# The three passes of a split matrix product, taken with the low weights first

## The chip, the cores and the metric

The kernel runs on one core of one Trainium2 chip. Its time is that of one execution on the device in microseconds (us); lower is better. TensorE (PE) multiplies, VectorE (DVE) and ScalarE (ACT) work on elements, GpSimd (POOL) does very little here, and the DMA queues are fed by SyncE (SP) and in part by ScalarE.

## The reference, cut to what matters

Two transformer-like blocks work on 256 tokens of width 1024 in float32. The first has two layers, and each of them is

```
h = modulate(rms_norm(x, norm_mix), shift1, scale1)
q, k, v, hy, g = split(h @ w_in)
x_mix = (sig(g_a) * (attention(q, k, v) @ w_o_attn) + sig(g_h) * (hyena(hy) @ w_o_hyena)) @ w_out
x = x + gate1 * x_mix
g, u = split(modulate(rms_norm(x, norm_ffn), shift2, scale2) @ w_gate_up)
x = x + gate2 * ((silu(g) * u) @ w_down)
```

In the first layer 256 context tokens take the same way beside the 256 tokens, so that a product there has 512 columns; in the second layer it has 256. The second block has a mixer (`w_in_2`, `w_out_2`), a cross attention (`w_xq_2`, `w_xk_2`, `w_xv_2`, `w_xo_2`) and 32 experts, of which each token takes two.

## The kernel before, in words

Every weight of the dense products is read once, as 128x128 blocks, 8 blocks (a unit of 512 KB) per DMA, into a ring of six slots. A dense product is made of float32r matmuls, and each float32 operand is split into two float32r parts, a high one and a low one. For a unit of weights ScalarE copies the high part into `his` (line 431, three slots), and VectorE then subtracts it from the unit in place, which leaves the low part in `ring_r` (line 439). The activations have been split in the same way: `HH_r` and `H_r` are the high and low part of most inputs, `VT_r` and `YF_r` those of the input of `w_down`; other tiles, `area_r` and `KF_r` among them, serve for the remaining ones. In the names of the profile the first name behind the arrow is the moving tile (activations) and the second the stationary tile (weights): `bank<-HH_r,his_r` is high weights with high activations, `bank<-H_r,his_r` high weights with low activations, `bank<-HH_r,ring_r` low weights with high activations.

The product of one 128x128 block is then a **trio** of matmuls that add into the same PSUM bank; low with low is left out. Each matmul has a weight load (LDWEIGHTS, PEld) of its own. Three functions write such trios:

- `pe_block` (line 460): one output bank, 4 or 8 blocks one after the other, the activations changing with each block. It makes the products of `w_in`, `w_o_attn`, `w_o_hyena`, `w_out`, `w_gate_up`, and most of the second block's.
- `pe_pair` (line 475): two output banks side by side, so that two trios in turn use the same activations. It makes the first two heads and the first pair of gate and up of each layer.
- `three` in `pe_down` (line 1608): four output banks, so that four trios in turn use the same activations (the blocks n = 0 to 3 of one k).

Four other places write their trios by themselves (lines 927, 1833, 1974, 2104).

Before a trio TensorE waits until the activations are there and until the low part of the unit is there (`ve_lo`, which VectorE counts up at line 439, after the high part). Nothing is waited for inside a trio. When the last matmul of a block product has ended, `pe_products` goes up; that lets ScalarE and VectorE take the bank, lets ScalarE overwrite the slot of `his` (line 431), and lets SyncE load the next unit into the slot of the ring. The order of the instructions on each engine is written out by hand in the program. Column sums by ones (lines 499 and 909) and small products stand between some blocks.

The experts at the end are plain float32 products from other slots. A branch behind them (`overflowing`) is taken only when an expert has more than 32 tokens: it then loads all experts a second time, 32 x 12 loads of 512 KB through a single slot (lines 2690 and following).

Of the kernel before, what the change touches and what calls it, by code (L numbers as in the profile page):

```python
# [267 lines left out]
def two_blocks_kernel(nc, T):  # L268
    ctx = ExitStack()
    with ctx:  # L270
# [145 lines left out]
        def hi_slot(n):  # L416
            return his[:, (n % NHI) * UF:(n % NHI + 1) * UF]

        def lo_slot(i):
            r = i % NS  # L420
            return ringr[:, r * UF:(r + 1) * UF]
# [21 lines left out]
        def pe_block(pe, key, out, name, l, b0, nk, moving, ready, step=1, n=1, turned=False, signals_end=True):  # L443
            for k in range(nk):
                w, i = stream.block(name, l, b0 + step * k, n)
                ready(k)
                if name in SPLIT:
                    pe.wait_ge(*ve_lo.at(nth[i]))
                    c = ((b0 + step * k) % UB) * P
                    whi, wlo = hi_slot(nth[i])[:, c:c + n * P], lo_slot(i)[:, c:c + n * P]  # L450
                    xhi, xlo = moving(k)
                    three = ((whi, xhi), (whi, xlo), (wlo, xhi))
                else:
                    pe.wait_ge(*stream.arrived(i))
                    three = ((w, moving(k)),)
                for m, (a, b) in enumerate(three):
                    end = k == nk - 1 and m == len(three) - 1
                    if turned:
                        a, b = b, a
                    ins = pe.eng.matmul(out, a, b, start=k == 0 and m == 0, stop=end)  # L460
                stream.spent[i] = (pe_products, key)
            if signals_end:
                ins.then_inc(*pe_products.up(*key))


        def pe_pair(pe, blocks, name, l, moving, ready):
            for k in range(8):
                ready(k)
                xhi, xlo = moving(k)
                for key, out, b0 in blocks:  # L470
                    w, i = stream.block(name, l, b0 + k)
                    pe.wait_ge(*ve_lo.at(nth[i]))
                    whi, wlo = hi_slot(nth[i])[:, k * P:k * P + P], lo_slot(i)[:, k * P:k * P + P]
                    for m, (a, b) in enumerate(((whi, xhi), (whi, xlo), (wlo, xhi))):
                        ins = pe.eng.matmul(out, a, b, start=k + m == 0, stop=k == 7 and m == 2)  # L475
                    stream.spent[i] = (pe_products, key)
                    if k == 7:
                        ins.then_inc(*pe_products.up(*key))

        def unit(name, l, b):  # L480
            return where[name, l, b // UB]
# [6 lines left out]
        def pe_open(pe, site, read_by=None, root_read_by=None):  # L488
            banks.hold(read_by or (ve_norm, ("used", site)), "sum", site)
            rsts.take(root_read_by or (pe_sums, ("spread", site)), site)  # L490
# [13 lines left out]
        def pe_added(site):  # L504
            for n in range(7):
                squares.take((ve_squares, ("added", site, max(n, 1))), site, n)
            squares.take((pe_sums, (site, 7)), site, 7)

        def pe_sum_seven(pe, site, cols):
            pe.wait_ge(*ve_squares.at("added", site, 6))  # L510
            pe.wait_ge(*banks.emptied("sum", site))
            for tb in range(cols // P):
                ins = pe.eng.matmul(banks.ap("sum", site)[:, tb:tb + 1], seven[:, tb * P:(tb + 1) * P], ones[:, 0:1], start=tb == 0,
                                    stop=False)
            ins.then_inc(*pe_sums.up(site, "seven"))

        def pe_sum_last(pe, site, cols):
            pe.wait_ge(*ac_squares.at(site, 7))
            for tb in range(cols // P):
                ins = pe.eng.matmul(banks.ap("sum", site)[:, tb:tb + 1], squares.ap(site, 7)[:, tb * P:(tb + 1) * P], ones[:, 0:1],  # L520
                                    start=False, stop=tb == cols // P - 1)
            ins.then_inc(*pe_sums.up(site, 7))
# [9 lines left out]
        def pe_spread(pe, site, cols, give=True):  # L532
            pe.wait_ge(*landed["con"])
            pe.wait_ge(*ve_norm.at("rstd", site))
            for tb in range(cols // P):
                ins = pe.eng.matmul(banks.ap("sum", site)[:, tb * P:(tb + 1) * P],
                                    rsts.ap(site)[:, tb:tb + 1].to_broadcast([P, P]), ident, start=True, stop=True)
            ins.then_inc(*pe_sums.up("spread", site))
            if give:
                banks.give("sum", site)  # L540


        def pe_idle(pe, site, n):
            out = banks.take((pe_sums, ("idle", site)), "idle", site)
            pe.wait_ge(*banks.emptied("idle", site))
            pe.wait_ge(*gp_start.at("ones"))
            for i in range(n):
                ins = pe.eng.matmul(out[:, 0:P], ones[:, :], ones[:, :], start=True, stop=True)
            ins.then_inc(*pe_sums.up("idle", site))
# [325 lines left out]
        def tokens(l):  # L875
            return 256 if l else 512
# [13 lines left out]
        def pe_head(pe, l, i):  # L890
            b, cols, _, _ = heads(l)[i]
            out = head_bank(pe, l, i)
            pe_block(pe, ("head", l, i), out[:, 0:cols], "w_in", l, 8 * pos[b], 8, lambda k: (HH[:, k, 0:cols], HL[:, k, 0:cols]),
                     lambda k: pe.wait_ge(*ve_norm.at("low", f"mix{l}", k)))
# [684 lines left out]
        def down_site(l):  # L1579
            return "final" if l else "mix1"  # L1580
# [12 lines left out]
        def cut_place(tile, m, t):  # L1593
            return tile[:, m % 4, 0:t]

        def pe_down(pe, l):
            t, site = tokens(l), down_site(l)
            pe_added(site)

            def three(half, k, n):  # L1600
                m, b = 22 * half + k, 88 * half + 4 * k + n
                u, c = unit("w_down", l, b), (b % UB) * P
                hi, lo = cut_place(VTR, m, t), cut_place(YFR, m, t)
                pe.wait_ge(*ve_cut.at("ff", l, m))
                pe.wait_ge(*ve_lo.at(nth[u]))
                whi, wlo = hi_slot(nth[u])[:, c:c + P], lo_slot(u)[:, c:c + P]
                for i, (w, x) in enumerate(((whi, hi), (whi, lo), (wlo, hi))):
                    ins = pe.eng.matmul(banks.ap("ff", l, 4 * half + n)[:, 0:t], w, x, start=k == 0 and i == 0, stop=k == 21 and i == 2)  # L1608
                return ins, u

            for half in range(2):
                for n in range(4):
                    banks.hold((ve_out, ("ff", l, 4 * half + n, t // 256 - 1)), "ff", l, 4 * half + n)
                for n in range(4):
                    pe.wait_ge(*banks.emptied("ff", l, 4 * half + n))
                for k in range(19 if half else 22):
                    for n in range(4):
                        ins, u = three(half, k, n)
                        if k == 21 and n < 3:
                            ins.then_inc(*pe_products.up("ff", l, half, n))  # L1620
                    ins.then_inc(*pe_products.up("down", l, half, k))
                    stream.spent[u] = (pe_products, ("down", l, half, k))
                if half:
                    for n in range(4):
                        for k in range(19, 22):
                            ins, u = three(half, k, n)
                            stream.spent[u] = (pe_products, ("down", l, 1, 21))
                        ins.then_inc(*pe_products.up("ff", l, half, n) if n < 3 else pe_products.up("down", l, 1, 21))
                for n in range(4):
                    banks.give("ff", l, 4 * half + n)  # L1630
            if l == 0:
                pe_open(pe, site)
                pe_sum_seven(pe, site, t)
                pe_sum_last(pe, site, t)
                pe_spread(pe, site, t)
                pe_idle(pe, site, 14)
# [1400 lines left out]
```

## Time and profile before

| | |
|---|---|
| Median of 3 executions | 2082.93 us (2081.61 to 2088.01) |
| Profiled execution, first to last instruction | 2084.6 us |
| TensorE busy | 1889.2 us, 91%, 14150 matmuls |
| VectorE busy | 1156.6 us, 55% |
| ScalarE busy | 903.5 us, 43% |
| DMA | 428.01 MB |

The busy time of TensorE counts from the first start to the last end of matmuls that overlap each other, so the time from one start to the next is shorter than the "mean ns" of one. No figure stands beside the span for what lies around it. Of the three executions without the profiler one is above the span and two are below it.

### The profile page before, as it was taken

How to read it: one execution, taken by the hardware profiler on the slowest of the kernel's cores; microseconds unless marked ns; L12 is line 12 of the kernel's file. 1: busy time of each engine (PE TensorE's matmuls, PEld its weight loads, DVE VectorE, ACT ScalarE, POOL GpSimd, SP SyncE). 2: the span in 40 equal slices, each digit the busy share in tenths (PEclk: the TensorE clock that was granted, in tenths of full speed). 3: DMA queues.
4: the chain of work that ended last, by engine and by line, in shares of the span. 5: the costliest groups of instructions: out<-in, count | busy, mean ns of one | idle time of the engine just before them, and what ended most of it. 6: DMA issues, size and time to landing. Idle time of an engine off the chain costs nothing.

```text
span 2084.6 us, 33760 instructions
## 1 busy us (share of the span) xinstructions
PE 1889.2 (91%) x14150; PEld 1554.0 (75%) x14150; DVE 1156.6 (55%) x1898; ACT 903.5 (43%) x1532; POOL 16.9 (1%) x31
## 2 busy tenths in 40 slices
PE   7999989999999999999899999999999767776666
PEld 4877668888778888798699999997898544454344
DVE  3555757776887788567656667689755111111012
ACT  4333345665756677455445555634844000000001
POOL 0000000000000000000000000000000000000000
PEclk8999999999999999999999999999999998999987
DMA  8222024553555555234055555543247999999995
GB/s 319 85 71 81 1 76 158 183 179 105 180 179 177 188 193 170 91 102 142 11 182 192 182 183 184 173 162 112 90 144 325 420 420 420 419 419 420 420 421 236
DMA packets 91121, 428.01 MB, mean 205 GB/s; under 512 B 11089, under 2 KB 12754, under 8 KB 66002
## 3 DMA queue, kind: packets, MB, share of 16 engines
q1 hardware_dynamic: 78866, 382.51, 49.3%
q10 hardware_dynamic: 12096, 43.26, 6.2%
q8 instruction: 114, 1.87, 0.4%
q14 instruction: 45, 0.37, 0.1%
HBM read 424.68 MB, written 1.05 MB: 204 GB/s over the span
## 4 chain that ended last, share of the span: by engine, by line
PE 64%; DMA 20%; DVE 8%; ACT 5%; issue 2%; SPq 1%; ACTq 0%; POOL 0%; DVEq 0%; POOLq 0%
PE bank L460 41%; PE bank L1608 8%; DMA area<-in_w 8%; DMA his<-in_w 4%; DMA ring<-in_w 4%; DMA PPT<-in_w 3%; PE bank L475 2%; PE bank L2497 2%; PE bank L2453 1%; DVE st L1259 1%; PE bank L1187 1%; PE bank L2104 1%; PE bank L927 1%; ACT PPT L1204 1%; DVE ring_r L439 1%
## 5 line engine op out<-in xcount | busy, mean ns | idle before, releaser
L439 DVE TENSOR_TENSOR ring_r<-ring,his_r 128x1024 fp32r<-128x1024 f32 x314 | 383.5, 1223 | 226.9 <-ACT his_r L431 225.5
L460 PE MATMUL bank<-HH_r,his_r 128*128 128x256 f32 (+1 forms) x1504 | 499.1, 332 | 1.4 <-DVE ring_r L439 1.4
L460 PE MATMUL bank<-HH_r,ring_r 128*128 128x256 f32 (+1 forms) x1504 | 492.2, 327 | 0.0
L460 PE MATMUL bank<-H_r,his_r 128*128 128x256 f32 (+1 forms) x1440 | 472.8, 328 | 0.0
L431 ACT ACTIVATE his_r<-ring 128x1024 fp32r<-128x1024 f32 x314 | 330.6, 1055 | 303.5 <-PE bank L460 273.4
L460 PEld LDWEIGHTS bank<-HH_r,his_r 128*128 128x128 f32 x1504 | 284.1, 189 | 35.2 <-issue 8.6
L460 PEld LDWEIGHTS bank<-HH_r,ring_r 128*128 128x128 f32 x1504 | 283.7, 189 | 25.1
L460 PEld LDWEIGHTS bank<-H_r,his_r 128*128 128x128 f32 x1440 | 270.7, 188 | 27.0 <-issue 1.0
L2469 DVE TENSOR_TENSOR tmp<-tmp,bank 128x128 f32<-128x128 f32 x64 | 18.4, 288 | 385.9 <-ACT tmp L2462 262.7
L460 PE MATMUL bank<-area_r,his_r 128*128 128x256 f32 (+1 forms) x480 | 148.8, 322 | 0.0
L2453 PE MATMUL bank<-area,KF 128*32 128x128 f32 x1888 | 86.1, 312 | 44.3 <-DMA area<-in_w 39.3
L1608 PE MATMUL bank<-VT_r,ring_r 128*128 128x512 f32 (+1 forms) x352 | 118.6, 337 | 0.0
L1608 PE MATMUL bank<-YF_r,his_r 128*128 128x512 f32 (+1 forms) x352 | 118.1, 336 | 0.0
L1608 PE MATMUL bank<-VT_r,his_r 128*128 128x512 f32 (+1 forms) x352 | 117.5, 334 | 0.0
L2453 PEld LDWEIGHTS bank<-area,KF 128*32 128x32 f32 x1888 | 70.6, 125 | 58.2 <-DMA area<-in_w 49.9
L460 PEld LDWEIGHTS bank<-area_r,his_r 128*128 128x128 f32 x480 | 90.1, 190 | 7.4
L2508 ACT ACTIVATE H<-bank 128x512 f32<-128x512 f32 x16 | 9.6, 597 | 191.3 <-PE bank L2497 191.3
L709 ACT ACTIVATE rst<-rst 128x1024 f32<-128x1024 f32 x80 | 83.6, 1045 | 1.6 <-DVE rst L701 1.6
L2497 PE MATMUL bank<-area,tmp 128*32 128x512 f32 x256 | 56.9, 646 | 20.1 <-DMA area<-in_w 19.5
L1335 ACT ACTIVATE VT_r<-area 128x512 fp32r<-128x512 f32 (+1 forms) x96 | 49.9, 523 | 51.0 <-PE bank L1608 45.3
L1608 PEld LDWEIGHTS bank<-YF_r,his_r 128*128 128x128 f32 x352 | 66.1, 188 | 7.7
L1608 PEld LDWEIGHTS bank<-VT_r,his_r 128*128 128x128 f32 x352 | 65.9, 187 | 7.6 <-DVE YF_r L1339 0.2
(415 smaller groups left out, 3301.0 us busy)
## 6 DMA issues: line engine op xcount, KB each, us to landing
area<-in_w SPq DMA_DIRECT2D x91, 1024.0 KB, 27.3
ring<-in_w_in SPq DMA_DIRECT2D x102, 512.0 KB, 3.5
ring<-in_w_gate_up SPq DMA_DIRECT2D x88, 512.0 KB, 3.5
ring<-in_w SPq DMA_DIRECT2D x36, 1024.0 KB, 27.4
HH<-in_w SPq DMA_DIRECT2D x26, 1024.0 KB, 26.8
ring<-in_w_down SPq DMA_DIRECT2D x44, 512.0 KB, 3.5
KX<-in_w_mod_rows ACTq DMA_DIRECT2D x28, 512.0 KB, 3.5
VX<-in_w_mod_rows ACTq DMA_DIRECT2D x28, 512.0 KB, 3.5
```

Of the source, the lines that this page charges most:

```text
L431: ac.eng.activation(hi_slot(n), stream.slot(u), ACT.Copy).then_inc(*ac_hi.up(n))
L439: ve.eng.tensor_tensor(lo_slot(u), stream.slot(u), hi_slot(n).bitcast(F32), ALU.subtract).then_inc(*ve_lo.up(n))
L460: ins = pe.eng.matmul(out, a, b, start=k == 0 and m == 0, stop=end)
L475: ins = pe.eng.matmul(out, a, b, start=k + m == 0, stop=k == 7 and m == 2)
L709: ac.eng.activation(prod, prod, ACT.Copy, accum_out=MODS[l][:, j, s:s + 1]).then_inc(*ac_mod.up("sum", n, s))
L927: ins = pe.eng.matmul(vb[tb // 2][:, o:o + 256], x[:, k, sl], w, start=k == 0 and n == 0 and o == 0, stop=k == 7 and n == 2 and o > 0)
L1187: ins = pe.eng.matmul(out[:, 0:256], vs(kc), c.pts[g % 2][:, kc * 256:(kc + 1) * 256], start=kc == 0, stop=kc == c.nk - 1)
L1204: ac.eng.activation(p[:, m * w:(m + 1) * w], src[:, m * w:(m + 1) * w], ACT.Exp, bias=st[:, so + m:so + m + 1], scale=c.rq(h, i + m) if c. ...
L1335: ac.eng.activation(hi, src, ACT.Copy).then_inc(*ac_cut.up(*key))
L1608: ins = pe.eng.matmul(banks.ap("ff", l, 4 * half + n)[:, 0:t], w, x, start=k == 0 and i == 0, stop=k == 21 and i == 2)
L2453: ins = pe.eng.matmul(out[32 * n:32 * n + 32, 0:P], HG[g % 2][:, k, 32 * j:32 * j + 32], w, start=k == 0, stop=k == 7, tile_position=(0, 3 ...
L2497: ins = pe.eng.matmul(out[32 * j:32 * j + 32, :], AT[j][:, 32 * k:32 * k + 32], w, start=k == 0, stop=k == 3, tile_position=(0, 32 * j))
```

## The change

In three functions the order of the passes of a trio becomes: low weights with high activations, high weights with high activations, high weights with low activations. Written as (weights, activations), `(whi, xhi), (whi, xlo), (wlo, xhi)` is turned by one place into `(wlo, xhi), (whi, xhi), (whi, xlo)`. `start` stays on the first matmul of a product and `stop` on the last one.

```diff
--- before.py
+++ after.py
@@ -449,7 +449,7 @@
                     c = ((b0 + step * k) % UB) * P
                     whi, wlo = hi_slot(nth[i])[:, c:c + n * P], lo_slot(i)[:, c:c + n * P]
                     xhi, xlo = moving(k)
-                    three = ((whi, xhi), (whi, xlo), (wlo, xhi))
+                    three = ((wlo, xhi), (whi, xhi), (whi, xlo))
                 else:
                     pe.wait_ge(*stream.arrived(i))
                     three = ((w, moving(k)),)
@@ -471,7 +471,7 @@
                     w, i = stream.block(name, l, b0 + k)
                     pe.wait_ge(*ve_lo.at(nth[i]))
                     whi, wlo = hi_slot(nth[i])[:, k * P:k * P + P], lo_slot(i)[:, k * P:k * P + P]
-                    for m, (a, b) in enumerate(((whi, xhi), (whi, xlo), (wlo, xhi))):
+                    for m, (a, b) in enumerate(((wlo, xhi), (whi, xhi), (whi, xlo))):
                         ins = pe.eng.matmul(out, a, b, start=k + m == 0, stop=k == 7 and m == 2)
                     stream.spent[i] = (pe_products, key)
                     if k == 7:
@@ -1604,7 +1604,7 @@
                 pe.wait_ge(*ve_cut.at("ff", l, m))
                 pe.wait_ge(*ve_lo.at(nth[u]))
                 whi, wlo = hi_slot(nth[u])[:, c:c + P], lo_slot(u)[:, c:c + P]
-                for i, (w, x) in enumerate(((whi, hi), (whi, lo), (wlo, hi))):
+                for i, (w, x) in enumerate(((wlo, hi), (whi, hi), (whi, lo))):
                     ins = pe.eng.matmul(banks.ap("ff", l, 4 * half + n)[:, 0:t], w, x, start=k == 0 and i == 0, stop=k == 21 and i == 2)
                 return ins, u
```

It touches 1888 trios of line 460, 64 of line 475 and 352 of line 1608, 6912 matmuls in all. DVE, ACT, POOL and SP have the same instructions in the same order; on PE each wait stands at the same place in the row of matmuls, and the count of matmuls is the same.

On PE, the start of the first block of `pe_block` in layer 0, behind the sums over columns of line 499 (bank0 is the output, `[waits ...]` what the matmul waits for). Before:

```order
L499 MATMUL bank5<-ones,tmp1 128x1 x3
L460 MATMUL bank0<-HH_r_50,his_r_62 128x512 [waits ve_lo,ve_mod]
L460 MATMUL bank0<-H_r_49,his_r_62 128x512
L460 MATMUL bank0<-HH_r_50,ring_r_61 128x512
L460 MATMUL bank0<-HH_r_50,his_r_62 128x512
L460 MATMUL bank0<-H_r_49,his_r_62 128x512
L460 MATMUL bank0<-HH_r_50,ring_r_61 128x512
```

After:

```order
L499 MATMUL bank5<-ones,tmp1 128x1 x3
L460 MATMUL bank0<-HH_r_50,ring_r_61 128x512 [waits ve_lo,ve_mod]
L460 MATMUL bank0<-HH_r_50,his_r_62 128x512
L460 MATMUL bank0<-H_r_49,his_r_62 128x512
L460 MATMUL bank0<-HH_r_50,ring_r_61 128x512
L460 MATMUL bank0<-HH_r_50,his_r_62 128x512
L460 MATMUL bank0<-H_r_49,his_r_62 128x512
```

The matmul that carries the wait was high with high and is now low with high. Inside the block the pair of matmuls with the same `his` tile stays a pair, and at the seam between two trios the `ring_r` pass has gone from in front of it to behind it.

On PE, the start of the down products of layer 0, line 1608 (bank2 and bank6 are two of the four outputs). Before:

```order
L1608 MATMUL bank2<-VT_r_54,his_r_62 128x512 [waits ve_out,ve_cut,ve_lo]
L1608 MATMUL bank2<-YF_r_55,his_r_62 128x512
L1608 MATMUL bank2<-VT_r_54,ring_r_61 128x512
L1608 MATMUL bank6<-VT_r_54,his_r_62 128x512
L1608 MATMUL bank6<-YF_r_55,his_r_62 128x512
L1608 MATMUL bank6<-VT_r_54,ring_r_61 128x512
```

After:

```order
L1608 MATMUL bank2<-VT_r_54,ring_r_61 128x512 [waits ve_out,ve_cut,ve_lo]
L1608 MATMUL bank2<-VT_r_54,his_r_62 128x512
L1608 MATMUL bank2<-YF_r_55,his_r_62 128x512
L1608 MATMUL bank6<-VT_r_54,ring_r_61 128x512
L1608 MATMUL bank6<-VT_r_54,his_r_62 128x512
L1608 MATMUL bank6<-YF_r_55,his_r_62 128x512
```

Here the waits are again on the first matmul. Before, the matmul behind a `ring_r` pass was high with high of the next bank; now it is high with high of the same bank.

## Rows read from the trace of the kernel before

**Rows 1.** The page, its head and busy times of the engines.

```profile
span 2084.6 us, 33760 instructions
PE 1889.2 (91%) x14150; PEld 1554.0 (75%) x14150; DVE 1156.6 (55%) x1898; ACT 903.5 (43%) x1532; POOL 16.9 (1%) x31
```

**Rows 2.** The page, chain that ended last, shares by line.

```profile
PE bank L460 41%; PE bank L1608 8%; DMA area<-in_w 8%; DMA his<-in_w 4%; DMA ring<-in_w 4%; DMA PPT<-in_w 3%; PE bank L475 2%; PE bank L2497 2%; PE bank L2453 1%; DVE st L1259 1%; PE bank L1187 1%; PE bank L2104 1%; PE bank L927 1%; ACT PPT L1204 1%; DVE ring_r L439 1%
```

**Rows 3.** Windows, both parts of the span; columns in the first line.

```profile
core 0: us, PE busy (x) PEld busy (x) DVE busy (x) ACT busy (x) POOL busy (x), PEclk, DMA share, GB/s
0.00:1500.00 1500.00, 1451.85 (x8292) 1234.78 (x8293) 1034.36 (x1594) 812.43 (x1351) 16.93 (x31) 0.99 0.43 143
1500.00:2085.00 585.00, 437.33 (x5861) 319.19 (x5859) 122.20 (x304) 91.07 (x181) 0.00 (x0) 0.92 0.89 365
```

**Rows 4.** Waits; us in total, times, longest us.

```profile
PE bank L460 <- DVE ring_r L439: 3.7, 4, 1.3
PE bank L475 <- DVE H_r L868: 0.7, 2, 0.4
...
ACT his_r L431 <- PE bank L460: 273.4, 150, 5.9
```

**Rows 5.** Chain of waits in time; start us, us, what, count.

```profile
626.04 131.85 PE bank L460 x576
757.90 116.75 PE bank L1608 x510
...
1150.08 68.08 PE bank L460 x576
...
1270.38 56.80 PE bank L1608 x480
```

**Rows 6.** Timeline of PE in the down products; start us, us, engine, line.

```profile
819.99 0.39 PE L1608 MATMUL bank<-VT_r,ring_r 128*128 128x512 f32 x1
820.22 0.39 PE L1608 MATMUL bank<-VT_r,his_r 128*128 128x512 f32 x1
820.45 0.39 PE L1608 MATMUL bank<-YF_r,his_r 128*128 128x512 f32 x1
820.68 0.39 PE L1608 MATMUL bank<-VT_r,ring_r 128*128 128x512 f32 x1
```

**Rows 7.** Lines by form; count, busy us, mean ns, idle before.

```profile
L460 PE MATMUL bank<-HH_r,his_r 128*128 128x512 f32 x624 | 247.5, 397 | 0.2 <-DVE ring_r L439 0.2
L460 PE MATMUL bank<-HH_r,ring_r 128*128 128x512 f32 x624 | 245.5, 393 | 0.0
L460 PE MATMUL bank<-H_r,his_r 128*128 128x512 f32 x624 | 244.8, 392 | 0.0
L460 PE MATMUL bank<-HH_r,his_r 128*128 128x256 f32 x880 | 251.6, 286 | 1.2 <-DVE ring_r L439 1.2
L460 PE MATMUL bank<-HH_r,ring_r 128*128 128x256 f32 x880 | 246.8, 280 | 0.0
L460 PE MATMUL bank<-H_r,his_r 128*128 128x256 f32 x816 | 228.0, 279 | 0.0
```

**Rows 8.** Timeline of PE where a block follows column sums.

```profile
63.52 0.36 PE L499 MATMUL bank<-ones,tmp 128*128 128x1 f32 x2
63.74 0.47 PE L460 MATMUL bank<-HH_r,his_r 128*128 128x512 f32 x1
64.06 0.39 PE L460 MATMUL bank<-H_r,his_r 128*128 128x512 f32 x1
64.29 0.39 PE L460 MATMUL bank<-HH_r,ring_r 128*128 128x512 f32 x1
```

**Rows 9.** Windows of TensorE, two neighbouring stretches.

```profile
core 0: us, PE busy (x), PEclk, DMA share, GB/s
119.20:122.60 3.40, 3.40 (x10) 0.50 0.25 98
122.60:126.00 3.40, 3.40 (x16) 1.00 0.00 0
```

**Rows 10.** The page, granted clock; DMA issue, KB each, us to landing.

```profile
PEclk8999999999999999999999999999999998999987
...
ring<-in_w_gate_up SPq DMA_DIRECT2D x88, 512.0 KB, 3.5
```

## The prediction

> **What bounds the kernel now.** I read four views in this order: the head of the page, the chain that ended last, the waits of TensorE, and then its timeline down to single matmuls. The head gives a span of 2084.6 us with TensorE busy for 91% of it [rows 1]. The chain says where that matters: 41% of the span hangs on line 460, 8% on line 1608 and 2% on line 475, the three functions that change, and the DMA entries in it belong to the experts at the end [rows 2]. The windows part the span in two. Up to 1500 us TensorE is busy for 1451.85 of 1500.00 us, with DMA at 0.43; behind it DMA is at 0.89 [rows 3]. The changed matmuls lie nearly all in the first part, where every nanosecond between two matmul starts is on the path. The second part starts when the first has ended (its first loads wait for TensorE's products), so what the first gains or loses is passed on whole.
>
> Next, what the first part waits for. Line 460 waited for a low part of weights 4 times, 3.7 us in all, the longest 1.3 us, and line 475 waited 0.7 us for an activation [rows 4]. ScalarE in its turn waited 273.4 us for line 460 to give a slot of `his` back [rows 4]. So ScalarE and VectorE are held back by TensorE and not the reverse, and the time of the products is their number times the step from one start to the next. That step is what the reader is to see in the chain: 131.85/576 = 228.9 ns for 512 columns in line 460, 116.75/510 = 228.9 ns in line 1608; for 256 columns 68.08/576 = 118.2 ns and 56.80/480 = 118.3 ns [rows 5].
>
> **The change part by part.** Nothing is removed or added: 2304 trios (1888 + 64 + 352) of three matmuls and three weight loads stay as many. The trios are turned by one place. I take four terms.
>
> *Waits in front of a trio.* The wait for the low part stands ahead of the trio in both versions, although only the low pass needs it. The low pass now comes first and so needs at once what had been waited for already. The 3.7 us and 0.7 us [rows 4] stay: 0 us. Would the old order have let high passes run ahead of that wait, the new one would lose up to these 3.7 us; it didn't, since the wait is on the high matmul, so 3.7 us is no end of my range. The slots of `his` and of the ring, and the banks, are given back on the last matmul of a block product, which comes at the same place: ScalarE's 273.4 us of waiting and the loads keep their times, 0 us.
>
> *New neighbours.* Inside a trio the step from high-high to high-low is unchanged. Of the other two, one now goes between two trios and one inside. In line 460 the `ring_r` pass was followed by other weights with another activation tile; now it is followed by other weights with the same tile `xhi`. Does a matmul go faster or slower behind one that streamed the same activations? Line 1608 answers it in the trace of before, because there three trios of four are followed by a trio with the same activations. The single steps from `VT_r,ring_r` to `VT_r,his_r`, to `YF_r,his_r` and to `VT_r,ring_r` are 0.23, 0.23 and 0.23 us [rows 6]. The long pieces are finer: with no such neighbour in line 460 and 0.75 per trio in line 1608 the mean steps are 228.9 and 228.9 ns, and 118.2 and 118.3 ns [rows 5]. Unrounded, the larger difference is 118.33 - 118.19 = 0.14 ns per matmul, or 0.14 x 3 / 0.75 = 0.56 ns per neighbour. The change makes 1888 new ones in line 460 and some 88 in line 1608: 1976 x 0.56 ns = 1.1 us at the most, 0 at the least. I take 0, since at 512 columns the rows show none.
>
> *First matmul of a row of them.* Behind sums over columns or another interruption the first matmul takes longer until the second starts: 64.06 - 63.74 = 0.32 us, against 64.29 - 64.06 = 0.23 us for the next [rows 8]. This falls on the high-high pass, as it stands first, and is seen in its mean: 397 ns against 393 and 392 at 512 columns, 286 against 280 and 279 at 256 [rows 7]. So (397 - 392.5) x 624 = 2.8 us and (286 - 279.5) x 880 = 5.7 us, together 8.5 us. In the new order the low pass stands first. I expect the 8.5 us to pass to `ring_r` whole: 0 us in sum. No row shows such a start with two different weight tiles behind each other, so both ends are open: -8.5 us if the penalty belonged to the pair that shares its weights, +8.5 us if it is paid a second time. By the nearest row, a start is 0.09 us longer than a step; that looks like an empty pipeline, which no choice of tile fills, and I take 0.
>
> *Last matmul of a product.* It was low with high, now it is high with low: 393 against 392 ns at 512 columns and 280 against 279 at 256 [rows 7]. Whoever waits for the bank waits 1 ns less, a few hundred times: under 0.5 us, taken as 0.
>
> Sum against the profiled execution: 2084.6 + 0 + 0 + 0 + 0 = 2084.6 us of span, with ends at 2076.1 and 2094.2 if both open terms went one way. The median of the executions shown is 2082.93 us, 1.7 us under that span, and I give the forecast on the scale of the median: **2083 us**. The three executions lie 6.4 us apart, about 0.3%; that is also what a measurement of this kernel can tell from no change.
>
> **The clock, which neither version rules.** In the granted clock nearly every slice up to 1500 us is at 9 tenths [rows 10], and a stretch at 0.50, that is 1.2 GHz, costs what two neighbouring windows show: 10 matmuls in 3.40 us against 16 at 2.4 GHz [rows 9], so 3.40 x 6/16 = 1.3 us. Before that stretch TensorE had waited between head sums. The change leaves these idle times as they are.
> The Trainium skill, TensorE: Matmul & The Clock Gate, section "What's actually happening", says that the point at which the clock changes is not tied to the kernel's start and differs from run to run. By that rule the same program gets such a stretch in one run and misses it in another; one trace can't show whether that is so.
>
> **The rivals.**
>
> *A. The start is paid twice (slower).* At each interruption the second matmul, too, now brings a new weight tile, while before it reused the first one's. If the extra time comes from loading the second tile and not from an empty pipeline, it comes on top. Price: 8.5 us more, 2083 + 8.5 = 2091.5 us, 0.4% slower. It decides when `HH_r,his_r` keeps its 286 and 397 ns and `HH_r,ring_r` rises to them. For it: the second load starts early only in a running row. Against it: in a running row new and old weights take the same step [rows 6].
>
> *B. The start gets cheaper (faster).* If the extra were the price of loading the same tile twice at a start, it would be gone: 2083 - 8.5 = 2074.5 us. Nothing in the rows speaks for it but that every such start in them had that pair [rows 8].
>
> *C. The clock falls otherwise (either sign).* To be told from nothing it takes 6.3 us, or five stretches of 1.3 us more or less than before: 2089.5 or 2076.5 us. For it: a later start by a fraction of a step could move such stretches. Against it: the executions shown span 6.4 us in all, and the median damps it.
>
> *D. Another rounding sends a token elsewhere (slower).* The sums are now added in another order, and the choice of experts hangs on the last digits. If an expert went over 32 tokens, the branch behind the experts would be taken: 384 loads of 512 KB through one slot, at 3.5 us each [rows 10] 1344 us, so some 3430 us. Against it: the DMA issues of before list no load into `rst`, the tile of that branch, so it wasn't taken; an expert near the limit and a token near a tie would both be needed.
>
> *E. The change doesn't do what it says.* The order on TensorE shows it in all three functions, and four places (lines 927, 1833, 1974, 2104) are left in the old order. That changes nothing in the sum, as every term above is for the three alone.
>
> **How the numbers follow.** Forecast (no change) 0.90; A 0.03; B 0.02; C 0.04, half on each side; D and E together under 0.01. Faster by over 0.3%: B and half of C, 0.04. Slower by over 0.3%: A, half of C and D, 0.05. Within: 0.91. The range takes the spread of the executions shown (2081.6 to 2088.0) and the small open terms, and reaches part of the way to A and B, from 2078 to 2089 us; beyond it lie A, B and D whole and the outer part of C, under 0.1 together.
>
> **What the profile of the changed kernel would show.** If I am right: the steps of the long pieces stay at 228.9 and 118.2 ns; `HH_r,his_r` falls to about 393 and 280 ns while `HH_r,ring_r` rises to about 397 and 286; the waits of line 460 for `ring_r` stay near 3.7 us and those of ScalarE for line 460 near 273 us. Wrong would be a step in line 460 that moves by more than 1 ns (5664 matmuls make 5.7 us of it), `his_r` means that stay up, or more idle time ahead of line 460.

## The result and the profile after

The changed kernel takes 2090.93 us (median of 19 executions, 2084.65 to 2094.45), the kernel before 2084.84 us (median of 19, 2081.61 to 2088.01). The ratio is 1.0022 with a 95% interval of 1.0015 to 1.0029: 0.2% slower, about 4.6 us. (The plain difference of the two medians is 6.1 us; this text goes by the ratio and its interval.) The forecast was no change, 2083 us, with 2078 to 2089 as its range; the median lies outside it, and the small slowdown is clear of the noise.

The head of the page after, which answers to [rows 1]:

```profile
span 2089.7 us, 33760 instructions
PE 1895.4 (91%) x14150; PEld 1555.7 (74%) x14150; DVE 1156.7 (55%) x1898; ACT 903.7 (43%) x1532; POOL 17.0 (1%) x31
```

TensorE is busy 6.2 us longer with the same 14150 matmuls; VectorE and ScalarE are as before. The chain of waits after, in the order of time (start us, us, what, count), answers to [rows 5] and shows three more pieces than stood there:

```profile
53.26 11.41 PE bank L927 x96
306.67 190.49 PE bank L460 x816
631.51 131.85 PE bank L460 x576
763.37 116.75 PE bank L1608 x510
906.94 11.42 PE bank L927 x96
1157.03 67.84 PE bank L460 x576
1277.08 56.81 PE bank L1608 x480
```

and the pieces of before at the places that moved:

```profile
52.10 11.00 PE bank L927 x96
304.98 187.28 PE bank L460 x816
901.47 11.00 PE bank L927 x96
```

The rows that the prediction had looked at keep their time to within 0.24 us. One row of 816 matmuls in line 460, the merge and `w_out` of layer 0, takes 190.49 - 187.28 = 3.2 us more. The two rows of line 927 take 0.4 us more each, though their code wasn't changed. The two profiled spans are 5.1 us apart: 3.2 us of it is this row, 0.8 us line 927, and 1.2 us stood there before any change could act, as the first changed matmul starts at 39.13 us before and at 40.29 us after. The slower row is slower all along. Windows of 25 us in it (us, PE busy and count of matmuls, granted clock, DMA), before:

```profile
320.00:345.00 25.00, 25.00 (x111) 1.00 0.53 170
400.00:425.00 25.00, 25.00 (x111) 1.00 0.58 187
```

after:

```profile
320.00:345.00 25.00, 25.00 (x109) 1.00 0.47 160
400.00:425.00 25.00, 25.00 (x109) 1.00 0.55 189
```

111 against 109 matmuls, at the same granted clock of 1.00 and with TensorE never idle. From start to start (the trace keeps them to the ns) these are 228.9 and 233.3 ns. (A window also counts matmuls that only reach into it: 25 us hold 109.2 or 107.2 such steps, and the count is 2 higher in both.) Most of the matmuls in the windows are gate products of `pe_block`, and matmuls with the same tiles (`HH_r`, `H_r`), the same 512 columns and the same new order ran at 228.9 ns in the row at 631 us. So it is a **pace that a row keeps**, and not the cost of a pass. The experiments look for what sets it.

What else was forecast, by form and by waits, answers to [rows 7] and [rows 4]:

```profile
L460 PE MATMUL bank<-HH_r,ring_r 128*128 128x256 f32 x880 | 250.8, 285 | 1.2 <-DVE ring_r L439 1.2
L460 PE MATMUL bank<-HH_r,ring_r 128*128 128x512 f32 x624 | 248.1, 398 | 0.7 <-DVE ring_r L439 0.7
L460 PE MATMUL bank<-H_r,his_r 128*128 128x512 f32 x624 | 246.4, 395 | 0.0
L460 PE MATMUL bank<-HH_r,his_r 128*128 128x256 f32 x880 | 246.4, 280 | 0.0
L460 PE MATMUL bank<-HH_r,his_r 128*128 128x512 f32 x624 | 245.3, 393 | 0.0
```

```profile
PE bank L460 <- DVE ring_r L439: 4.3, 4, 1.4
...
ACT his_r L431 <- PE bank L460: 275.8, 151, 5.9
```

The price of the first matmul went from `his_r` (now 280 and 393 ns) to `ring_r` (285 and 398), as forecast, and the waits stay within 0.6 and 2.4 us. Beyond the forecast only `H_r,his_r` at 512 columns has grown, from 392 to 395 ns.

### The profile page after: what moved, and what is told of

Its sections match the earlier page's. It is cut to its first block, busy times and chain, and to the rows that moved or that the text cites. A ratio compares the mean times of both kernels' runs of the same rounds, so it can differ in the third digit from the quotient of the medians.

```text
span 2089.7 us, 33760 instructions
## 1 busy us (share of the span) xinstructions
PE 1895.4 (91%) x14150; PEld 1555.7 (74%) x14150; DVE 1156.7 (55%) x1898; ACT 903.7 (43%) x1532; POOL 17.0 (1%) x31
## 4 chain that ended last, share of the span: by engine, by line
PE 64%; DMA 20%; DVE 8%; ACT 5%; issue 2%; SPq 1%; ACTq 0%; DVEq 0%; POOL 0%
PE bank L460 41%; PE bank L1608 8%; DMA area<-in_w 8%; DMA his<-in_w 4%; DMA ring<-in_w 4%; DMA PPT<-in_w 3%; PE bank L475 2%; PE bank L2497 2%; PE bank L2453 1%; DVE st L1259 1%; PE bank L1187 1%; PE bank L2104 1%; PE bank L927 1%; ACT PPT L1204 1%; DVE ring_r L439 1%
## 5 line engine op out<-in xcount | busy, mean ns | idle before, releaser
L460 PE MATMUL bank<-HH_r,ring_r 128*128 128x256 f32 (+1 forms) x1504 | 498.9, 332 | 1.9 <-DVE ring_r L439 1.9
L460 PE MATMUL bank<-HH_r,his_r 128*128 128x256 f32 (+1 forms) x1504 | 491.7, 327 | 0.0
L460 PE MATMUL bank<-H_r,his_r 128*128 128x256 f32 (+1 forms) x1440 | 474.3, 329 | 0.0
L431 ACT ACTIVATE his_r<-ring 128x1024 fp32r<-128x1024 f32 x314 | 330.8, 1056 | 306.9 <-PE bank L460 275.8
L460 PEld LDWEIGHTS bank<-HH_r,ring_r 128*128 128x128 f32 x1504 | 283.6, 189 | 35.7 <-issue 9.0
L460 PEld LDWEIGHTS bank<-HH_r,his_r 128*128 128x128 f32 x1504 | 283.6, 189 | 27.7 <-issue 1.0
L460 PEld LDWEIGHTS bank<-H_r,his_r 128*128 128x128 f32 x1440 | 270.8, 188 | 25.3
L460 PE MATMUL bank<-area_r,his_r 128*128 128x256 f32 (+1 forms) x480 | 149.4, 324 | 0.0
L460 PEld LDWEIGHTS bank<-area_r,his_r 128*128 128x128 f32 x480 | 90.0, 190 | 7.8
L2497 PE MATMUL bank<-area,tmp 128*32 128x512 f32 x256 | 62.6, 682 | 21.4 <-DMA area<-in_w 20.7
L2462 ACT ACTIVATE tmp<-bank 128x128 f32<-128x128 f32 x32 | 8.9, 278 | 145.7 <-PE bank L2453 145.7
```

What stands on the lines that cost most here:

```text
L431: ac.eng.activation(hi_slot(n), stream.slot(u), ACT.Copy).then_inc(*ac_hi.up(n))
L2497: ins = pe.eng.matmul(out[32 * j:32 * j + 32, :], AT[j][:, 32 * k:32 * k + 32], w, start=k == 0, stop=k == 3, tile_position=(0, 32 * j))
```

## The experiments

Sixteen runs were profiled and timed, two of them (e1, e5) without an edit. The table gives the piece of the chain for the row of 816, and the ratio to the kernel before with its 95% interval. Some of the expectations give 186.5 and 189.8 us for this row, which is counted from the start of its second matmul to the start of its last; 187.2 to 187.4 and 190.5 us are the same two cases as pieces of the chain. The row's time in the table is that of one profiled execution per kernel.

| kernel | row, us | ratio |
|---|---|---|
| before | 187.28 | 1 |
| changed | 190.49 | 1.0022 (1.0015 to 1.0029) |
| e1 before again | 187.20 | 0.9996 (0.9981 to 1.0010) |
| e2 line 460 alone | 190.48 | 1.0009 (0.9996 to 1.0023) |
| e3 line 475 alone | 187.28 | 1.0004 (0.9987 to 1.0020) |
| e4 line 1608 alone | 187.20 | 1.0005 (0.9992 to 1.0018) |
| e5 changed again | 190.49 | 1.0017 (1.0007 to 1.0027) |
| e6 changed, old order in attention and hyena of layer 0 | 187.28 | 1.0009 (0.9998 to 1.0019) |
| e7 before, 48 matmuls new | 190.51 | 1.0015 (1.0003 to 1.0027) |
| e8 changed, nudge | see below | 1.0017 (1.0007 to 1.0027) |
| e9 changed, 12 matmuls old | 187.38 | 1.0002 (0.9993 to 1.0011) |
| e10 before, 12 matmuls new | 187.26 | 1.0003 (0.9992 to 1.0014) |
| e11 order hl, hh, lh | 190.48 | 1.0022 (1.0012 to 1.0033) |
| e12 order lh, hl, hh | 187.28 | 1.0004 (0.9992 to 1.0016) |
| e13 order hh, lh, hl | 190.48 | 1.0031 (1.0019 to 1.0042) |
| e14 order hl, lh, hh | 190.48 | 1.0013 (1.0003 to 1.0022) |
| e15 changed, tiles exchanged | 190.54 | 1.0003 (0.9992 to 1.0015) |
| e16 before, tiles exchanged | 188.77 | 1.0007 (0.9994 to 1.0020) |

(In the orders, the first letter is the weights and the second the activations; h is the high part, l the low one.)

**Is it the program or chance? Which function?** e1 is the kernel before once more, without an edit.

> The kernel before, unchanged, a second time. In the profile of the changed kernel the long row of line 460 that starts near 306 us (816 matmuls, layer 0, merge) takes 190.49 us instead of 187.28, about 233.3 ns per matmul instead of 228.9, and the 96 matmuls of line 927 take 11.41 us instead of 11.00, twice, although line 927 was not changed. Theory 1 (the pace is set by the program): this profile shows the old paces again, 187.3 us and 11.00 us twice, and the time is that of before, ratio 1.000. Theory 2 (the pace of a row of matmuls is drawn anew in each execution): one or more of these rows, or another one, comes at the other pace here, and the profile is 3 us or more away from 2084.6.

The row takes 187.20 us and the ratio holds 1: theory 1. But the first piece of line 927 took 11.41 us here and the second 11.02, with the same program that had 11.00 twice. So those rows are drawn by chance, and the 0.8 us of them above isn't the change's. Theory 1 holds for the long row, theory 2 for the short ones.

e2, e3 and e4 change one function each.

```diff
-                    three = ((whi, xhi), (whi, xlo), (wlo, xhi))
+                    three = ((wlo, xhi), (whi, xhi), (whi, xlo))
```

> The new order in line 460 alone (1888 of 2304 trios). Theory 1: if the pass order inside a row sets the pace of that row, the row of 816 matmuls near 306 us takes 190.5 us and the ratio is about 1.0015 to 1.002 (3.2 us and a bit of 2085); the rows of line 927, which follow line 475 and not line 460, stay at 11.00 us. Theory 2: no fixed relation, ratio within 0.0005 of 1.

The row takes 190.48 us, as theory 1 says. The ratio of 1.0009 is low, and its interval holds both 1 and 1.0015.

```diff
-                    for m, (a, b) in enumerate(((whi, xhi), (whi, xlo), (wlo, xhi))):
+                    for m, (a, b) in enumerate(((wlo, xhi), (whi, xhi), (whi, xlo))):
```

> The new order in line 475 alone (64 trios). Theory 1 in its form that a row takes its pace from what stands in front of it: line 927 follows line 475 and a few column sums, so both of its rows go to 11.41 us, and the ratio is about 1.0004 (0.8 us). If the pace comes from the order inside a row: 11.00 us twice and ratio 1.000. Theory 2: either, with no relation to the change.

```diff
-                for i, (w, x) in enumerate(((whi, hi), (whi, lo), (wlo, hi))):
+                for i, (w, x) in enumerate(((wlo, hi), (whi, hi), (whi, lo))):
```

> The new order in line 1608 alone (352 trios). In the profile of the changed kernel these rows kept their pace (116.75 us for 510 matmuls, 56.8 us for 480). Theory 1: ratio 1.000, all rows as before. Theory 2: another row may come at the other pace, without relation to the change.

187.28 and 187.20 us: neither function makes the row. Line 927 took 11.41 us twice in both, so it has no relation to line 475 (e4 hasn't changed that one). The cause lies in line 460.

**Which products?** e5 is the changed kernel without an edit.

> The changed kernel a second time. In the four profiles just taken the row of 816 matmuls of line 460 that starts near 306 us ran at 229.1 or 229.2 ns per matmul in every kernel that keeps the old order in line 460 and at 233.1 in both that have the new one; the small rows of 24 to 96 matmuls with 256 columns took 113.3 or 117.8 ns with no relation to the change. Theory 3 (the pace of a long row is a state that the row falls into at its start and then keeps, and the order of the passes there decides which): 189.8 us for this row again and a ratio near 1.002. Rival (theory 2, drawn anew in each execution): about an even chance of 186.5 us.

190.49 us again, ratio 1.0017. Then the old order came back in the attention and hyena products of layer 0:

```diff
                     three = ((wlo, xhi), (whi, xhi), (whi, xlo))
+                    if key[0] in ("oa", "oh") and l == 0:
+                        three = ((whi, xhi), (whi, xlo), (wlo, xhi))
```

> The changed kernel with the old order only in the attention and hyena products of the merge of layer 0 (96 of the 2304 trios). Theory 3: the row of 816 falls into the faster pace again, 186.5 us instead of 189.8, and the kernel is 3.2 us faster than the changed one. Rival (theory 4: the new order is slower wherever a trio of the merge has it, here 64 gate trios per pair of columns): the gate products, which keep the new order, stay at 233.3 ns, and the row takes about 189 us.

187.28 us: the gate products keep the new order and run at 228.9 ns. Theory 4 falls.

```diff
                     three = ((whi, xhi), (whi, xlo), (wlo, xhi))
+                    if key in (("oa", 0, 0), ("oh", 0, 0), ("oh", 0, 1)):
+                        three = ((wlo, xhi), (whi, xhi), (whi, xlo))
```

> The kernel before with the new order only in the first attention product and the first two hyena products of layer 0: 16 trios, 48 matmuls, at the start of the row of 816. Theory 3: these 48 matmuls decide the pace of the whole row, 189.8 us instead of 186.5, 3.2 us from 48 matmuls. Rival (theory 4): only the 48 can change, by 4.4 ns each, 0.2 us.

190.51 us, but this isn't the proof it looks like: the row stood at 233.3 ns from its first trios on, ahead of any hyena product, which the changed kernel never did in its profiles. So the run can't show that the 48 matmuls set the pace. In the changed kernel the first attention product, with the same order and the same tiles, runs at 228.9 ns, so the pace at the start of this row can differ, too. What the run shows is that a row can be at the slower pace for nearly all of its 190 us with nothing but the old order behind the 48 matmuls.

```diff
                     pe.wait_ge(*banks.emptied(key, l, j))
+                    for _ in range(4 if (key, l, j) == ("ga", 0, 1) else 0):
+                        pe.eng.matmul(out[:, 0:1], ones[:, :], ones[:, 0:1], start=True, stop=True)
```

> The changed kernel with four matmuls of one column (ones with ones) in front of the gate product of column 1 of the merge in layer 0, inside the row of 816; their result is overwritten. Each row of 512 columns that starts behind such column sums ran at 228.9 ns in all six profiles. Theory 3: the row behind the nudge goes back to 228.9 ns, about 760 x 4.4 ns = 3.3 us are won for 0.3 us that the four cost, with the pass order as in the changed kernel. Rival (theory 4): 233.3 ns behind the nudge as before it, and the kernel is 0.3 us slower than the changed one.

Windows of e8 behind the nudge, which stands at 317.3 us, and 40 us later:

```profile
320.00:345.00 25.00, 25.00 (x111) 1.00 0.45 153
360.00:385.00 25.00, 25.00 (x109) 1.00 0.53 189
```

Behind the nudge the row goes back to 111 matmuls in 25 us, as in before, with the new order in every trio: theory 4 falls once more, and theory 3 is right that a pace is kept and can be reset. It is wrong on who sets it: from some 352 us on the pace was 233.3 ns again. That is where the hyena products of the next pair of columns stand. They, and not the start of the row, send it to the slower pace.

**What in the hyena product?** Two of its four activation blocks lie in the tile `tmp`, with their low parts in `area`. Around them the steps are uneven, in every profile. The last two trios of the second hyena product and the gate trios behind them, as steps from one start to the next in ns, worked out from the start times in the traces (t is `tmp`, a the low part in `area`, H and h the gate's activations, and - marks the low weights):

```
before            t233 a237 t-232 t235 a234 t-226  |  H234 h235 H-229 H232 h226 H-229
e12 lh, hl, hh    t-232 a238 t231 t-235 a235 t225  |  H-235 h235 H229 H-231 h226 H229
e9  12 old        t-232 t235 a228 t232 a233 t-232  |  H-238 H232 h231 H-226 H229 h232
changed           t-233 t235 a227 t-233 t234 a232  |  H-233 H233 h234 H-233 H233 h234
e11 hl, hh, lh    a233 t232 t-235 a228 t232 t-235  |  h231 H234 H-233 h233 H234 H-233
```

(These are the trios of the first pair of columns.) The steps 226, 229, 232 in turn are the pace of 228.9; 233, 233, 234 that of 233.3. Before goes into these trios at 233.3 (the first hyena product has sent it there) and leaves at 228.9. Changed stays. I first took the leaving step as the cause, and edited only the last trio of the second product, 12 matmuls in layer 0:

```diff
                     three = ((wlo, xhi), (whi, xhi), (whi, xlo))
+                    if key in (("oh", 0, 1), ("oh", 0, 3), ("oh", 0, 5), ("oh", 0, 7)) and k == nk - 1:
+                        three = ((whi, xhi), (whi, xlo), (wlo, xhi))
```

> The changed kernel with the old order only in the last trio of the second hyena product of each pair of columns in layer 0: 4 trios, 12 matmuls of 6912. In the profiles the matmuls with the tile tmp (hyena products, blocks 2 and 3) take uneven steps, and the row leaves them at 228.9 ns where the last one is low weights with tmp (a step of 226 ns), and at 233.3 ns where the last one is high weights with the low activations of area. Theory 5 (the pace of the row is set by the step that leaves tmp): the row of 816 matmuls is 3 us shorter than in the changed kernel, about 187.3 instead of 190.5 us. Rival (theory 6: it is the low pass in front, in all products of the merge): 190.5 us, as 12 matmuls are nothing.

187.38 us. Twelve of 6912 matmuls take the whole 3.1 us back, and the ratio is 1.0002. e10 is the mirror image: the kernel before, with the same condition and the new order under it.

> The counterpart: the kernel before with the new order only in those 4 trios. Theory 5: the row of 816 goes to 233.3 ns behind the first hyena products, about 190 us instead of 187.3, and the kernel is about 0.13% slower by 12 matmuls. Theory 6: 187.3 us.

187.26 us: theory 5 said 190. Its other old trio on `tmp` had been enough. So it is not the last step alone. e11 and e12 write all three functions in other orders:

```diff
-((whi, xhi), (whi, xlo), (wlo, xhi))
+((whi, xlo), (whi, xhi), (wlo, xhi))     e11
+((wlo, xhi), (whi, xlo), (whi, xhi))     e12
```

> A third order in all three functions: high weights with low activations, high with high, low with high. The low weights are last again, and so is tmp in a hyena product; high with high is not first. Theory 5: 187.3 us for the row of 816, ratio to before within 0.001 of 1. Rival (theory 7: the row is fast only in the one order of before): 190.5 us.

> A fourth order in all three functions: low weights with high activations, high with low, high with high. The low weights are first, as in the changed kernel, but the last matmul of a hyena product streams tmp again. Theory 5: 187.3 us for the row of 816. Theory 6: 190.5 us, ratio near 1.0017 as in the changed kernel.

```profile
303.35 190.48 PE bank L460 x816
```

```profile
304.17 187.28 PE bank L460 x816
```

e11 (first fence) has the slower pace and e12 (second) the faster one. Both end on `tmp`, so theory 5 falls; e12 has the low weights first as the changed kernel has, so theory 6 falls; e12 isn't the order of before, so theory 7 falls. What divides the four orders is theory 8: whether the activations go high, low, high (before, e12) or have the two high ones side by side (changed, e11). e9 and e10, which have one trio of each kind in the second product, fit as well: one trio that alternates is enough there. The last two orders were forecast by it:

```diff
+((whi, xhi), (wlo, xhi), (whi, xlo))     e13
+((whi, xlo), (wlo, xhi), (whi, xhi))     e14
```

> Fifth order in all three functions: high with high, low with high, high with low; so the activation tiles go high, high, low. Theory 8 (in a hyena product only trios whose activations alternate, high, low, high, bring a row at 233.3 ns back to 228.9): 190.5 us for the row of 816. Rival (theory 5, the row is fast when the last pass streams tmp): also 190.5 us, as the last pass streams area. Rival (theory 6, low weights first are slow): 187.3 us.

> Sixth order: high weights with low activations, low with high, high with high; activations low, high, high, and the last pass streams tmp. Theory 8: 190.5 us for the row of 816. Theory 5: 187.3 us. (e11, with the same order of activations, took 190.5.)

Both 190.48 us. All six orders are now run: the two that alternate give 187.28 us, the four that don't 190.5. "Alternate" is a name for what divides them and not yet a reason. Behind one another the tiles of a hyena product go t a t t a t in one case, and t t a t t a or a t t a t t in the other. So the orders also differ in where the row enters and leaves `tmp`, and in whether two neighbouring passes on `tmp` belong to one block or to two; no run tells these apart.

**Is it the tile?** e15 and e16 exchange places: `tmp` holds two blocks of the attention product, `VX` two of the hyena product.

```diff
-            return KFR[:, k, 0:t] if k < 4 else KXR[:, k - 4, 0:t] if k < 6 else VXR[:, k - 6, 0:t]
+            return KFR[:, k, 0:t] if k < 4 else KXR[:, k - 4, 0:t] if k < 6 else tmpr[k - 6][:, 0:t]
-            return HYR[:, 10 + k, 0:t] if k < 2 else tmpr[k - 2][:, 0:t]
+            return HYR[:, 10 + k, 0:t] if k < 2 else VXR[:, k - 2, 0:t]
```

> The changed kernel, but the high activations of hyena blocks 2 and 3 lie in VX, and those of attention blocks 6 and 7 in tmp, which is only an exchange of places. Theory 9 (the uneven steps come from streaming the tile tmp in turn with area): the hyena products have even steps, the last two blocks of each attention product have the uneven ones (227 to 238 ns), and the row then goes to 233.3 ns and stays, about 190.5 us. Rival (theory 10: the unevenness belongs to the hyena products, their data or their weights): the uneven steps stay in the hyena products.

190.54 us; the steps at the hyena products are even (233, 233, 234), and the uneven ones moved into the attention products. The ratio of 1.0003 doesn't show the 3.1 us, but its interval reaches up to 1.0015, which is 3.1 us: the times can't tell here, and the reading rests on the trace.

> The same exchange of places in the kernel before. Theories 8 and 9: the uneven steps are in the last two blocks of each attention product; each such product turns the pace over (228.9 to 233.3 ns or back), and as there are eight of them, one behind each other column without a hyena product between, the row is at the slower pace for about half its length, 189 us. Theory 10: uneven steps in the hyena products and 187.3 us.

This was the sharpest forecast. Windows of e16 behind the first, second, third and fourth attention product:

```profile
317.50:332.50 15.00, 15.00 (x66) 1.00 0.43 140
335.00:350.00 15.00, 15.00 (x67) 1.00 0.54 178
356.50:371.50 15.00, 15.00 (x66) 1.00 0.52 176
374.00:389.00 15.00, 15.00 (x67) 1.00 0.55 177
...
306.60 188.77 PE bank L460 x816
```

66, 67, 66, 67 matmuls in 15 us: each product with alternating activations on `tmp` turns the pace over, once to 233.3 and once back, and the row takes 188.77 us where 189 was forecast. Theory 9 holds. In the kernel before two such products stand behind each other in each pair of columns, so the pace is turned twice and the row stays at 228.9 ns but for about a dozen matmuls between.

The trace of e7 shows the same turning without an exchange of tiles. Its row came to the second pair of columns at 233.3 ns, and there the hyena products have the old order (behind the first product stand blocks whose high part lies in `area`, too):

```
e7, 2nd pair, 1st product   t232 a238 t-231 t235 a235 t-225  |  a235 a235 a-229 a231 a226 a-229
e7, 2nd pair, 2nd product   t233 a225 t-232 t226 a229 t-235  |  H227 h232 H-233 H233 h234 H-233
```

The first product turns the row to 228.9 ns and the second turns it back to 233.3, and the same happens in the third and fourth pair. That is why e7 took 190.51 us with the old order nearly everywhere: two turns leave a row at the pace at which it came, which was the slower one here and is the faster one in the kernel before. Products that don't alternate leave it at 233.3 ns whether it came at 228.9 (the changed kernel, first pair) or at 233.3 (its later pairs).

## Why the prediction was wrong, point by point

- **What bounds it**: right. Up to 1500 us the time is the number of matmuls times their step, and what the first part loses is passed on: 3.2 us in the step are 3.2 us in the chain.
- **Waits in front of a trio** (0 us): right, 4.3 against 3.7 us and 275.8 against 273.4 us; what moved is under 1 us on TensorE.
- **New neighbours** (0 us, 1.1 at the most): the step that failed. I priced a new neighbour by the mean step of two long rows, and both were rows without `tmp`. The sum then treated the step as a property of two matmuls that stand side by side, to be multiplied by their number. It is a pace that the row keeps: 16 trios on `tmp`, four in each pair of columns, decide for several hundred matmuls behind them. Measured: 4.4 ns on some 720 matmuls, 3.2 us, nearly all of it on matmuls far from the trios that cause it.
- **First matmul** (8.5 us pass over whole): right to 1 ns, 286 went over as 285 and 397 as 398. Neither rival A nor B happened, so the slowdown isn't A's although it has its sign. What A had for itself, that the second weight load starts early only in a running row, was a wrong reading: in the trace of before it starts at 63.83 us for the matmul at 64.06 behind column sums, and at 400.02 us for the one at 400.25 in a running row, 0.23 us ahead in both.
- **Last matmul of a product**: too small to see.
- **Clock and rounding** (rivals C and D): neither made the slowdown of the profiled execution. Up to 1500 us TensorE was at half clock for 41.0 us in the profile of before and for 34.1 us in that of after, so less and not more, and the kernel after runs the same 33760 instructions, without the second round of experts.
- **What was to prove it wrong**: I had written a step in line 460 that moves by more than 1 ns, and that is how it shows; but I looked for it in all of line 460, and it is 4.4 ns in one row and 0 in the others.
- **The range**: it held the shown part (2084.84 + 3.2 = 2088) but not the median. It stood on a median of three executions, 2082.93 us, and that of nineteen is 2084.84; these 1.9 us are about as much as the median lies above the upper end, so the miss of the range is in part this shift and not the change. The slowdown itself was not foreseen at all. What was missing is a rival for it: each of mine had its price at the start of a row or outside TensorE.

It stood in the trace of before. The piece 304.98 187.28 PE bank L460 x816 gives 229.5 ns, where the other rows of 512 columns give 228.9. Of these 0.6 x 816 = 0.5 us about half is the longer start of the first matmul and the end of the last one; the other half, 0.24 us, is the detour of the row at the hyena products (the mean step from the second start to the last is 229.2 ns). Its timeline there has steps up to 0.24 us, where the row has 0.22 and 0.23 us otherwise:

```profile
314.94 0.40 PE L460 MATMUL bank<-area_r,his_r 128*128 128x512 f32 x1
315.18 0.40 PE L460 MATMUL bank<-tmp_r,ring_r 128*128 128x512 f32 x1
315.41 0.40 PE L460 MATMUL bank<-tmp_r,his_r 128*128 128x512 f32 x1
315.65 0.40 PE L460 MATMUL bank<-area_r,his_r 128*128 128x512 f32 x1
315.88 0.39 PE L460 MATMUL bank<-tmp_r,ring_r 128*128 128x512 f32 x1
```

**What stays open.** The row explains 3.2 us, a ratio of 1.0015, which is the lower end of the first interval and inside that of e5 (1.0007 to 1.0027). Over all kernels the eight with the row at 190.5 us have a mean ratio of 1.0017 and the seven at 187.3 us one of 1.0003 (e8 and e16, between the two, left out), 0.0013 or 2.8 us apart, which agrees. Up to about 1.4 us of the 4.6 may be chance or something that no run here isolates. Why alternation on `tmp` turns the pace to and fro while two high tiles side by side only send it to 233.3 ns, and what in the place of `tmp` does it, wasn't settled; no run had these activations in a place of their own. How often the row starts at the slower pace, as in e7, isn't known either: it did in one of 18 profiles. And the effect was seen at 512 columns alone: in layer 1 the same row of 816 matmuls, with 256 columns and the same tiles, took 96.39 us before and 96.47 after. No order beat the kernel before.

## What to carry to other kernels

When an engine is busy without a gap, read the step from start to start for every long row by itself, not as a mean over a line: a change of a few matmuls can leave the row behind them at another pace. Before pricing a reorder at nothing, look in the old trace for places where the step is uneven, and ask which operands stand there and whether the new order passes them in the same turn. And of two kernels a few us apart, compare the pieces of the chain one by one, with the same program run twice beside them, since some rows change pace by chance.

## What the runs showed of the hardware

- Rows of float32r matmuls with a weight load each take one of two paces at the granted clock of 1.00 (2.4 GHz): 228.9 or 233.3 ns at 512 columns, 113.3 or 117.8 ns at 256. In these profiles a row kept its pace until it was interrupted or streamed the tile `tmp` in turn with `area`. At 256 columns the same program came with either: the two rows of line 927 took 11.00 and 11.00 us in the first profile of before, and 11.41 and 11.02 in the second; the row of 576 at some 1150 us took 65.53 us in e6 and e7 and 68.08 in before (other programs, but the same code in this row for e7). At 512 columns the long row followed the order of its passes in every profile but that of e7, which had the slower pace from its start.
- The Trainium skill, TensorE: Matmul & The Clock Gate, section "Back-to-back issue gap", gives N/2.4 + 2.5 ns for an isolated warm matmul, 216 ns at 512 columns, and about 131 ns for a sustained stream of weight loads and matmuls of 512 columns, whose spacing, it says, both operations set. The traces differ from the second figure: each of these matmuls has a weight load, and the step is 228.9 or 233.3 ns. The measurement decides here. Against the first figure the step is 13 or 17 ns longer; whether the weight loads make these ns, no run here shows.
- The stretches at half clock did differ between executions of one program: from 120.8 to 124.2 us the granted clock was 0.50 in the profile of the changed kernel (11 matmuls) and 1.00 in e5, the changed kernel again (17 matmuls). The Trainium skill, TensorE: Matmul & The Clock Gate, section "What's actually happening", says that the point of the change differs from run to run, and the two traces agree. It wasn't the cause, as the row of 816 had a granted clock of 1.00 in both kernels.
